# Earlier requests for table rows and dense tiles, six slots per retrieval, denser pieces and other homes for the last rows in a one-core decoder-layer kernel

## What is computed

```python
v1, i1 = lax.top_k(s1, PEER_TOPK)
v2, i2 = lax.top_k(s2, PEER_TOPK)
cand = (v1[..., :, None] + v2[..., None, :]).reshape(b, s, PEER_HEADS, PEER_TOPK * PEER_TOPK)
best, pos = lax.top_k(cand, PEER_TOPK)
expert_idx = jnp.take_along_axis(cand_idx, pos, axis=-1)
gates = jax.nn.softmax(best.astype(jnp.float32), axis=-1).astype(h.dtype)
u = jnp.take(u_tab, ix, axis=0)
act = jax.nn.gelu(jnp.einsum('chkd,cd->chk', u, hx), approximate=False)
vv = jnp.take(v_tab, ix, axis=0)
y = jnp.einsum('chk,chkd->cd', gx * act, vv)
```

## Time and profile before

| | before |
|---|---|
| median of three runs | 1761.15 us (1759.21 to 1764.15) |
| profiled execution | 1763.38 us, its span 1761.5 us |
| TensorE busy | 82% |
| VectorE busy | 68% |
| GpSimd busy | 40% |
| ScalarE busy | 31% |
| moved by DMA | 635.29 MB, mean 361 GB/s |
| of it GpSimd's queue | 446.76 MB, 64.6% of the DMA engines' time |
| of it SyncE's queue | 187.28 MB, 27.8% |

### The profile page before, as it was taken

One profiled execution on the slowest core, in us unless ns is written; L12 is line 12 of the kernel. 1 busy time (PEld: TensorE's weight loads), 2 busy tenths in 40 slices (PEclk: granted clock), 3 DMA queues, 4 the chain that ended last, 5 costly groups with the idle time before them and its releaser, 6 DMA issues.

```text
span 1761.5 us, 19725 instructions
## 1 busy us (share of the span) xinstructions
PE 1438.3 (82%) x7128; PEld 947.8 (54%) x7128; DVE 1198.8 (68%) x2102; ACT 542.4 (31%) x1585; POOL 700.6 (40%) x626
## 2 busy tenths in 40 slices
PE   2979999989999998889889476665797888777954
PEld 2658987878788875666666243343332333222321
DVE  5867886889889988888545467668644454554462
ACT  3003432764311256343210356536201010110132
POOL 1001011000122344555566656646554556554551
PEclk9889999999999999999999676767798989888978
DMA  9999998849969689999999999999999999998995
GB/s 340 386 386 406 403 360 309 305 172 367 358 228 368 238 305 387 382 382 402 372 409 362 373 386 371 384 358 351 375 409 397 395 375 410 405 416 345 414 406 230
DMA packets 148652, 635.29 MB, mean 361 GB/s; under 512 B 31516, under 2 KB 35794, under 8 KB 84050
## 3 DMA queue, kind: packets, MB, share of 16 engines
q0 software_dynamic: 82976, 446.76, 64.6%
q1 hardware_dynamic: 65580, 187.28, 27.8%
HBM read 789.15 MB, written 2.10 MB: 449 GB/s over the span
## 4 chain that ended last, share of the span: by engine, by line
PE 31%; DMA 31%; DVE 19%; POOL 8%; issue 6%; ACT 2%; SPq 2%; DVEq 1%; POOLq 0%; another core or an unknown queue 0%; ACTq 0%
DMA u_rows<-in_peer_u,expert 19%; DVE u_rows L2028 10%; PE ps L1162 7%; DMA v_rows<-in_peer_v,expert_rows 6%; PE ps L1064 5%; PE ps L1214 5%; POOL v_rows L798 5%; PE ps L456 4%; DVE first_acc L485 3%; PE ps L901 2%; DMA ring<-in_w_in 2%; PE ps L1129 2%; PE ps L907 2%; DMA ada_first<-in_w_ada 1%; POOL u_rows L798 1%
## 5 line engine op out<-in xcount | busy, mean ns | idle before, releaser
L2028 DVE SCALAR_TENSOR_TENSOR u_rows<-u_rows,h 128x1024 f32<-128x1024 f32 (+1 forms) x416 | 593.1, 1467 | 387.5 <-DMA u_rows<-in_peer_u,expert 338.2
L798 POOL DMA_INDIRECT u_rows<-in_peer_u,expert x256 | 336.5, 1315 | 357.4 <-DVE u_rows L2028 285.5
L1162 PE MATMUL ps<-v_rows,diag 128*32 128x512 f32 x1672 | 278.2, 734 | 124.9 <-DMA v_rows<-in_peer_v,expert_rows 89.7
L798 POOL DMA_INDIRECT v_rows<-in_peer_v,expert_rows x209 | 269.9, 1291 | 191.8 <-PE ps L1162 138.1
L1214 PE MATMUL ps<-dense_rows,dense_weight 128*128 128x512 f32 x576 | 258.7, 606 | 12.4 <-DVE dense_sums L2106 8.4
L456 PE MATMUL ps<-h2T,dense_rows 128*128 128x256 f32 x1152 | 256.3, 383 | 3.8 <-ACT dense_weight L1560 3.8
L456 PEld LDWEIGHTS ps<-h2T,dense_rows 128*128 128x128 f32 x1152 | 219.3, 192 | 47.8 <-issue 17.8
L1162 PEld LDWEIGHTS ps<-v_rows,diag 128*32 128x32 f32 x1672 | 71.3, 131 | 280.2 <-issue 279.7
L1214 PEld LDWEIGHTS ps<-dense_rows,dense_weight 128*128 128x128 f32 x576 | 109.2, 193 | 161.6 <-issue 161.6
L307 POOL DMA_DIRECT2D ada_late<-in_w_ada x61 | 32.4, 532 | 305.7 <-DVE ada_acc L321 263.7
L321 DVE SCALAR_TENSOR_TENSOR ada_acc<-ada_late,cact,ada_acc 128x2048 f32<-128x2048 f32 x57 | 133.8, 2347 | 16.2 <-DMA ada_late<-in_w_ada 15.0
(11 more groups left out here) (309 smaller groups left out, 1854.6 us busy)
## 6 DMA issues: line engine op xcount, KB each, us to landing
ada_late<-in_w_ada POOLq DMA_DIRECT2D x61, 1024.0 KB, 7.8
dense_rows<-in_dense_u SPq DMA_DIRECT2D x36, 1024.0 KB, 22.3
dense_rows<-in_dense_v SPq DMA_DIRECT2D x36, 1024.0 KB
ada_first<-in_w_ada SPq DMA_DIRECT2D x64, 512.0 KB, 11.7
ring<-in_w_in SPq DMA_DIRECT2D x10, 2048.0 KB, 24.8
ring<-in_w_o SPq DMA_DIRECT2D x8, 2048.0 KB, 14.1
ring<-in_w_peer_q SPq DMA_DIRECT2D x8, 2048.0 KB, 15.2
opened<-in_w_in SPq DMA_DIRECT2D x8, 1024.0 KB, 13.0
```

The costliest lines, as they stand in the source:

```text
L798: nc.gpsimd.indirect_dma_start(buf[:, :], None, table, bass.IndirectOffsetOnAxis(ap=places, axis=0), bounds_check=last_sparse, oob_is_err= ...
L1162: ins = nc.tensor.matmul(ps[rows, k, :], diag[n % len(diag)][:, :], v_slot(n)[0][:, 512 * k:512 * k + 512], start=first, stop=last)
L2028: ins = nc.vector.scalar_tensor_tensor(out=u_rows[b][:, lo:hi], in0=u_rows[b][:, lo:hi], scalar=1.0, in1=h2[:, q // H, lo:hi], op0=ALU.mul ...
```

## The change

Five things are changed. None adds or removes work.

1. `retrieval_slots`: each job's 17 parts are spread over six slots, from slot 6q - 6. Before it was five slots for jobs 1 to 7 and four for jobs 8 to 15; the last job ended with slot 66 and now ends with slot 89.
2. `gather_key` and `gather_v`: v rows 0 and 1 are due behind u row 17 (before 24), rows 2 and 3 behind 20 and rows 4 and 5 behind 21 (before 31). Rows 2 and 3 wait for the first half of w_pq3 and no longer for all of it.
3. SyncE asks for dense tile 3, and behind it tile 4, when the first half of w_pq2 is read, and no longer when bank p5 is full.
4. `piece_key`: a dense piece every 2.5 slots and no longer every 2.6, from slot 158: the last at slot 245 (before 249). The spreading of the final gain comes at 249 (before 255), and its four rows use the four banks 6, 7, 4 and 5, where they used 4 and 5 twice.
5. Homes at the end: rows 248 to 251 go to `u_rows`, and 252 to 255 to `v_rows`. `TAIL_FREE` is 249 (before 254).

```diff
-    plan([f"g2b{g}" for g in range(4)] + [f"fg{g}" for g in range(4)], [4, 5])
+    plan([f"g2b{g}" for g in range(4)] + ["fg2", "fg3"], [4, 5])
...
+    plan(["fg0", "fg1"], [6, 7])
...
-    TAIL_FREE = 254
+    TAIL_FREE = 249
+    FROM_U = range(TAIL + 8, TAIL + 12)
...
         if n < 2:
-            return 24
+            return 17
         if n < len(v_rows):
-            return 31
-        if n >= LAST:
+            return 20 + n // 4
+        if n >= TAIL + 6:
             return SLOTS
-        if TAIL <= n < TAIL + 6:
+        if TAIL <= n:
             return TAIL_FREE + (n - TAIL) // 4
...
-        key = max(TAIL_FREE if n >= TAIL else 0, group_order(n // QUADS) + n % QUADS - ahead)
+        key = group_order(n // QUADS) + n % QUADS - ahead
...
-        return 158 + 13 * j // 5
+        return 158 + 5 * j // 2
...
-        return (5 * q - 5, 5) if q < H else (5 * H - 5 + 4 * (q - H), 4)
+        return 6 * q - 6, 6
...
-    for n in list(range(TAIL)) + list(range(TAIL + 4, LAST)):
+    for n in list(range(TAIL)) + [n for n in range(TAIL + 4, SLOTS) if n not in FROM_U]:
...
-        if n >= LAST:
-            b = n - LAST
+        if n in FROM_U:
+            b = n - FROM_U[0]
...
                 if s == 3:
-                    full(sp, "p5")
+                    sp.wait_ge(q_half_read, 3)
...
                 if n == 2:
+                    pool.wait_ge(q_half_read, 4)
+                if n == 4:
                     full(pool, "p7")
...
-                if n >= LAST:
-                    pool.wait_ge(dots, n + 1)
+                if n in FROM_U:
+                    pool.wait_ge(dots, LAST + n - FROM_U[0] + 1)
...
-                if n == piece_key(DENSE - 1) + 6:
+                if n == piece_key(DENSE - 1) + 4:
...
-                if n == piece_key(DENSE - 1) + 7:
+                if n == piece_key(DENSE - 1) + 5:
```

## The result

The changed kernel is slower. Its median is 1782.09 us (1779.78 to 1783.94), beside 1762.65 for the kernel before on the same chip (1759.21 to 1766.29): a ratio of 1.010, interval 1.0075 to 1.0125, or 19.4 us. The forecast was 1764 with a range of 1748 to 1779. The profiled execution took 1780.38 us, its span is 1778.5.

The account below looks back on a forecast made before the run. The prediction took the DMA queues as the bound, after a stretch of idle DMA at 565 to 668 us. Its terms +7 - 4 + 2 - 2 = +3 on the median of 1761.15 gave 1764 us, range 1748 to 1779.

Parts of the forecast that it names:

- GpSimd's new waits: GpSimd's queue: second-table row 0 asked for at about 578 to 579 after a 9 us wait, row 2 about 594.4.
- The dots lose what six slots gain: VectorE up to slot 28: 9.9 us lost to GpSimd's waits against 8 gained; about +1 us, from -4 to +4.
- ScalarE, PE, row group 0: Retrieval jobs 4 and 5: exponents at 614.4 and 638.8, dense tile 2 at 640.8, row group 0 ending about 668.
- Bytes: DMA in 565 to 668 us: 3 MB less moved than before; +7 us taken, bounds -7.5 and +15.
- Lighter slots: VectorE from slot 36 on: four slots take 15.6 us, formerly 19.0, so DMA runs fuller; -4 us, from -9 to 0.
- distance shrinks from 8 us to 3 by 850: Sign to look for: from 700 us on, the lag behind the kernel before falls from 8 us to 3 by 850.
- Pieces: Dense pieces every 2.5 slots: two new boundaries where PE waits for VectorE; +2 us, from 0 to +8.
- The end: Last rows' homes and final gains: waits before row 249 and the last gain rows go; -2 us, from -5 to 0.
- Dense tiles sooner: Dense tiles 3 and 4 asked for about 7 us sooner, at 565, while the queue is not full; 0 us.
- the hole: Stretch 565 to 668 us, DMA engines 0.77 busy at 283 GB/s, with 23.7 us of idle DMA.
- rival A: Slower: PE's late start, dense tile 2 at about 641, keeps v-row releases and u rows late; +15 us, 1776; 22%.
- my first paragraph: What bounds the kernel: after the stretch 565 to 668 us it moves a fixed number of bytes at a fixed rate.

## Why the prediction was wrong

Point by point, by its own steps:

- *GpSimd's new waits*: right. Row 0 was forecast for 578 to 579 with a wait of about 9 us, and came at 578.63 with 9.54; row 2 for 594.4, and came at 594.20.
- *The dots lose what six slots gain*: right. By VectorE's timelines dot 28 starts at 633.20 in the kernel before, at 625.43 with six slots alone (7.8 us sooner, 8 were forecast) and at 636.96 in the changed kernel (3.8 us later; +1 was forecast, from -4 to +4). The losses came to 11.5 us, not 9.9.
- *ScalarE, PE, row group 0*: right to 2 us. Forecast 614.4, 638.8, 640.8 and 668 for the two exponents, dense tile 2 and the end of group 0; measured 616.23, 640.68, 642.83 and 669.10.
- *Bytes*: **this step failed.** It turned 20 us of late release into 3 MB and +7 us. The trace shows 5.4 MB in the same 103 us, 13.4 us. The step took "the same 20 first-table rows" for both kernels and one dense tile less. In fact GpSimd requested 33 rows in that window before and 26 after: the seven that are missing are v rows 6 to 9 and u rows 36 to 38, 23 first-table rows against 20. By the queues' bytes 3.3 MB of rows were not moved (the last of the 33 had not all landed by 668) and 2.0 MB of dense tiles, two tiles and not one: behind tiles 3 and 4 SyncE asked for four more there before (637.63 to 662.33) and for two after (658.65 and 665.56), as each waits for PE to be through with an older tile. GpSimd is in order: with v row 6 held until 669.40, nothing behind it leaves, and the queue ran dry (92 GB/s in 655 to 660). I had named u row 36 as late in the step before, and then left it and its followers out of the sum.
- *Lighter slots*, -4: the stretch 668 to 850 went at 384 GB/s where before had 381, (384 - 381) x 182 = 0.5 MB, 1.4 us. With the exponents moved it is 391, 4.6 us. Over all traces of this stretch the kernels with the old slots show 376 to 384, those with six slots 387 to 393 where group 0 begins by 655, and 374 to 385 where it begins at 665 or later. So the relief was there to be had and went with PE's late start. Why is not shown: GpSimd's waits for row groups there were 2.2 us before and 41.0 in the changed kernel (16.8 of them the one that ends at 669.40), but also 20.7 with the exponents moved. My forecast's "distance shrinks from 8 us to 3 by 850" did not happen; the lag stayed at 12 to 14.
- *Pieces*, +2 of 0 to +8: 7 us, near the bound that I had written down. **This term was mis-sized too.** The waits were not covered: 21.0 us in three where there had been 8.36 in one. I priced the boundaries by one trace of one boundary and discounted them for the full queue.
- *The end*, -2 of 0 to -5: 0 by the median, and too small to tell from -2 (interval -4 to +3 us). The chain there was a full queue, which I had at 98% busy and still took to give something.
- *Dense tiles sooner*, 0: they were not tried alone. The six-slot and early-row parts together with the pieces make 11.5 + 7 = 18.5 of the 19.4 us, each known to some 3 us, which leaves them nothing that could be measured.

So the sum with measured terms is +12 for the start (relief included), +7 for the pieces and 0 for the end: 19, where 19.4 was measured and +3 forecast. Of the 16 us between, the bytes of the hole are 6, the relief 3, the pieces 5 and the end 2. The start of rival A was what happened (PE's late start keeps the releases late, and in-order GpSimd holds the u rows too) and its +15 for the start less 4 of relief is 11. It had the pieces at 4 and not 7, which is most of what its +15 lacks of 19. I gave it 22% because "one group and two tiles are 17.7 us in a cycle of 20.6", so PE should win back the delay. PE did have that room; the queue did not. With the DMA engines 97% busy from 668 to 850 the lag of 11 to 14 us was still there at row 160, and stood at 18.7 at the end with that of the pieces: bytes not moved in the hole were time at the end. That sentence stood in my first paragraph, and the sum didn't follow it.

The Trainium skill ("Perfetto Trace Analysis", Optimization Strategy under Identifying Performance Opportunities) says to look for the gaps on the engine that ought to be full in a regime, and for what blocks it there. This case agrees: PE's waits of 16.23 and 8.17 us say little by themselves, and the 92 GB/s of the queues in 655 to 660, inside GpSimd's 16.85 us wait, name both the place and the blocker. The fit that the prediction cited from the Trainium skill ("DMA: Bandwidth & Descriptors", Anatomy of one DMA), 3.7 us for such a gather, is not met by any gather shown here. The prediction calls the 5.39 us of the earlier trace rows those of a gather alone, but they weren't: GpSimd sent three more, at 522.75, 524.05 and 525.34, before that one landed. In the full queue of the end a gather took 16.33 to 22.40 us.

## What to carry to other kernels

Where a saturated queue follows a hole, count every request that each issuing engine makes before the hole ends, in both versions, also those that only stand behind the late one in its list, and the other queue's too: the bytes that are missing, at the rate of the full queue, were the time here, and PE's slack did not give it back. Look also at what else stands behind a wait in a list written out by hand; two lines of ScalarE's list made six slots per retrieval and early rows cost 12 us together, and with them moved the whole change came out level. Asking sooner paid nothing here: rows 0 to 5, asked for 25 to 39 us earlier, gained nothing, and a last request sent 6.7 us sooner landed at the same time.

## What the runs showed of the hardware

In the full DMA queue of the end the last gather, of 0.742 MB, took 16.33 us to land in the kernel before, and 22.40, that is 6.1 us longer, where the request was sent 6.7 us sooner. In the changed kernel it took 21.04:

```profile
1743.23 21.04 DMA v_rows<-in_peer_v,expert_rows
```

PE's restart after an idle stretch doesn't grow with the idle time here. At 14.0 us for 64 matmuls the 96 of the dense tiles would take 21.0. They took 23.75 after 3.78 us idle, 22.70 after 8.17 in the changed kernel, 22.34 after 10.04 with early rows alone and 23.68 after 25.86 with job 4's exponent moved: 1.3 to 2.75 us more. In the changed kernel the granted clock behind the 8.17 us idle was 0.50 (1.2 GHz) from 642.80 to 645.00 and 1.00 (2.4 GHz) from 647.00 to 650.00; the mean of 640 to 650 hides this:

```profile
640.00:650.00 10.00, 7.17 (x25) 6.07 (x26) 9.39 (x20) 8.76 (x37) 3.19 (x3) 0.68 0.54 172
```
